# A decoder layer on one core: a second weight tile is multiplied during setup, and the first stage's small steps get new slots

## The chip, the cores and the metric

The kernel runs on one core of a Trainium2 chip. The metric is the device time of one execution in microseconds. Three runs of the kernel before took 1853.64, 1849.91 and 1853.60 us, median 1853.6. A difference of 0.2% is 3.7 us.

The engines: PE (TensorE) multiplies and writes PSUM, which has eight banks of 512 columns; ACT (ScalarE) and DVE (VectorE) read PSUM and SBUF; POOL (GpSimd) works in SBUF alone; SP (SyncE) issues most transfers.

## The reference

One inference step of one decoder layer, for a prompt of 1024 tokens and for 8 sequences of 4 tokens (the "samples"), 1056 columns in all, D = 1024:

```
ada = c @ w_ada + b_ada                      # shift, scale, gate for each norm
h = rmsnorm(x, g_norm1) * (1 + scale1) + shift1
z = h @ w_in                                 # q,k,v,o of two mixers, gates
qk = silu(causal conv of width 4 over q_a|k_a)
ha = mLSTM(q, k, v, input gate, log forget gate), normed per head
hb = gated linear attention(q, k, v, decays), normed per head
x = x + gate1 * ((sigmoid(g_a)*ha*sigmoid(o_a) + sigmoid(g_b)*hb*silu(r_b)) @ w_out)
x = x + gate2 * SwiGLU(rmsnorm(x, g_norm2) * (1 + scale2) + shift2)
```

All inputs and outputs are fp32. Each mixer has four heads. Outputs are the new x of both groups of tokens, normed, and the new states.

## The kernel before

**Products.** h is kept transposed, as eight chunks of 128 channels by 1056 tokens, and split in a high and a low part, each in the rounded fp32 format (`Hh`, `Hl`). So is every weight tile of 1024 x 128 (`Wh`, `Wl`). A product is Wh·Hh + Wh·Hl + Wl·Hh. A tile is multiplied in three thirds of the tokens (384, 320 and 352 columns, called pieces c = 0, 1, 2, one PSUM bank each) and two halves of the channels (h = 0, 1), so a half has 3 x 12 multiplications and a tile 72. Weights arrive as halves in four buffers (`raw`), ACT rounds a half to its high part (`split_hi`, L1326) and POOL subtracts to get the low part (`split_lo`, L1566).

**Setup** (`setup_phase`, L129 to L583). SP loads nine tiles of x rows, then `w_ada` in eight pieces of 1 MB (n = 0 to 7); behind piece 3 it issues four small strided loads for the tile "small" (gate columns and the rank-16 input), at the end the two halves of the weights of "q", and then it stores the transposed x. PE transposes x (L300), ACT squares its rows (L441) for the norm. PE multiplies the conditioning with each `w_ada` piece (`ada_part`, L337), ACT copies the sum out (`partial`, L447), PE turns it (`ada_columns`, L327). That happens four times, s = 0 to 3, and each gives shift and scale for two chunks of h. DVE then makes the multipliers (`affine`, L531), scales the chunk (`scaled`, L556: x times multiplier times the spread norm, which lies in PSUM), ACT adds the shift and rounds (`upper`, L454), DVE makes the low part (`lower`, L562). Between these, PE multiplies the first tile, "small", chunk by chunk as h is made (`first_upper`, `first_lower`, L350 and L362). Three times it multiplies the identity with itself instead (`keep_busy(8)`, L314).

**The mixer** (`mixer_phase`, L733) is a sequence of windows: S once, then A and B for each head, at the end L. Window S has the tiles small, q, k, v0, v1. A window's time is counted in slots, one slot for each piece of PE: `TIMELINE` lists piece after piece and, behind a piece, the small steps that `AT_SLOT` (L608) puts in that slot. Every engine goes through the same list in order and does its part of each entry. So the slot of a step is its place in each engine's queue. In S, slots 0 to 5 are small, 6 to 11 q, 12 to 17 k, 18 to 23 v0, 24 to 29 v1. ACT, at piece c = 0 of a half, splits the next half, and in the pieces of h = 1 it copies the finished bank out (`evacuate`, L1333). PE starts a tile's piece only when the bank's former content has been copied out (L1069 to L1070):

```
if h == 0:
    wait(pe, s_pfree[b], turns)
```

Banks 0 to 3 take turns by the number of the piece; small's pieces are 0 to 2, q's 3 to 5, k's 6 to 8, so k's second third lies in bank 3, where q's first was. The banks 4 to 7 serve the small steps.

**The small steps of S.** `rows` makes the rows of the gates: DVE adds the biases, ACT does exp and ln (L1424 to L1428), DVE sums and scans (`rows_stage`, L1949). `rows_exp` takes four exponentials on ACT (L1429). `rows_t` turns the rows on PE, DVE copies the columns, and SP stores the rows, which `decay_load` and `interq_load` read back. `conv_q`, `taps_q` and `silu_q` are the convolution (DVE), then tanh (ACT) and the product (DVE); the same for k. `vs0`, `vs1`, `vsum` are the values of the samples. Window A begins with its q tile; ACT and DVE make `decay` in slot 1 and ACT `alpha_hi` in slot 3.

Of the kernel before, what the change touches and what calls it, by code (L numbers as in the profile page):

```python
# [5 lines left out]
F32 = mybir.dt.float32  # L6
# [7 lines left out]
P = 128  # L14
# [114 lines left out]
def setup_phase(nc, g, a, block):  # L129

    with ExitStack() as ctx:
# [26 lines left out]
        ar = spare[:, 0:D].rearrange("p (j c) -> p j c", c=512)  # L158
# [14 lines left out]
        s_ssq, s_t, s_sqrt = sem("ssq_done"), sem("ms_done"), sem("sqrt_done")  # L173
# [6 lines left out]
        PARTB = (g.ps[4], g.ps[3])  # L180
# [10 lines left out]
        NQ = 256  # L191
        PARTS = [(0, 512), (512, 512), (SEQ, NS)]

        @block.sync
        def _(sp):
# [9 lines left out]
            for n in range(NA * KH):  # L205
# [15 lines left out]
            for h in range(2):  # L221
                sp.dma_start(g.raw[:, 2 + h], w_half(w_in, "S", 0, 1, h)).then_inc(g.s_w[2 + h], 16)
# [4 lines left out]
        def _(pool):  # L227
# [48 lines left out]
            pool.memset(g.nout[:, :], 0.0).then_inc(s_const, 1)  # L276
            for n in range(2):
# [3 lines left out]
            for n in range(2):  # L281
                pool.wait_ge(g.s_hi, n + 1)
                pool.tensor_tensor(g.Wl[:, n], by_parity(g.raw[:, n]), g.Wh[:, n].bitcast(F32), ALU.subtract).then_inc(g.s_lo, 1)

        @block.tensor
        def _(pe):
# [50 lines left out]
            def ada_part(n):  # L337
# [5 lines left out]
                if h == 0 and s >= 2:  # L343
                    pe.wait_ge(s_arow, s - 1)
                for k in range(KC // KH):
                    last = pe.matmul(PARTB[s % 2][CP * k:CP * (k + 1), :], cT[:, h * KC // KH + k, :], wpiece(n)[:, k, :],
# [3 lines left out]
            def first_upper(k, thirds):  # L350
# [3 lines left out]
                for m, w in enumerate((g.Wh, g.Wl)):  # L354
                    pe.wait_ge(g.s_lo if m else g.s_hi, h + 1)
                    for c in thirds:
                        if c == 2:
                            pe.wait_ge(g.s_hsh, h + 1)
                        pe.matmul(g.ps[c][:, 0:CUT[c + 1] - CUT[c]], slice_k(w[:, h], k % 4), g.Hh[:, k, CUT[c]:CUT[c + 1]],
                                  start=(k == 0 and m == 0), stop=False)  # L360

            def first_lower(k, thirds):  # L362
# [3 lines left out]
                for c in thirds:  # L366
                    if c == 2:
                        pe.wait_ge(g.s_hsl, h + 1)
                    last = pe.matmul(g.ps[c][:, 0:CUT[c + 1] - CUT[c]], slice_k(g.Wh[:, h], k % 4), g.Hl[:, k, CUT[c]:CUT[c + 1]],
                                     start=False, stop=(k == KC - 1))  # L370
                    if k == KC - 1 and c < NPC - 1:
                        last.then_inc(g.s_piece, 1)
                if k % 4 == 3 and 2 in thirds:
                    last.then_inc(g.s_used, 1)
            pe.wait_ge(s_trc, 1)
# [26 lines left out]
            first_upper(4, (0, 1))
            first_upper(5, (0, 1))
            ada_columns(3)
            for k in range(4):
                first_lower(k, (2,))
            first_lower(4, (0, 1))
            first_lower(5, (0, 1))
            keep_busy(8)
            first_upper(6, (0, 1))  # L410
            first_upper(7, (0, 1))
            for k in range(4, KC):
                first_upper(k, (2,))
# [2884 lines left out]
```

## Time and profile before

| | us |
|---|---|
| median of the three runs | 1853.6 |
| profiled execution, its span (first to last instruction) | 1851.7 |
| PE busy | 1815.7 |
| DVE, POOL, ACT busy | 1133.4, 776.4, 732.3 |

The profiled execution has no time of its own beside its span; what lies around the span is taken from the median of the runs. In the line of time of PE a multiplication of 128 columns and more is shown longer than its pitch, because multiplications are pipelined; the pitch is the difference of the starts. All times below are microseconds from the span's start.

### The profile page before, as it was taken

How to read it: one execution, taken by the hardware profiler on the slowest of the kernel's cores; microseconds unless marked ns; L12 is line 12 of the kernel's file. 1: busy time of each engine (PE TensorE's matmuls, PEld its weight loads, DVE VectorE, ACT ScalarE, POOL GpSimd, SP SyncE). 2: the span in 40 equal slices, each digit the busy share in tenths (PEclk: the TensorE clock that was granted, in tenths of full speed). 3: DMA queues.
4: the chain of work that ended last, by engine and by line, in shares of the span. 5: the costliest groups of instructions: out<-in, count | busy, mean ns of one | idle time of the engine just before them, and what ended most of it. 6: DMA issues, size and time to landing. Idle time of an engine off the chain costs nothing.

```text
span 1851.7 us, 36566 instructions
## 1 busy us (share of the span) xinstructions
PE 1815.7 (98%) x14652; PEld 1742.7 (94%) x14652; DVE 1133.4 (61%) x1960; ACT 732.3 (40%) x1528; POOL 776.4 (42%) x667
## 2 busy tenths in 40 slices
PE   7999999999999999999999999999999999999998
PEld 5899999999999999999989899989999999999998
DVE  6852746526474364753575688885675667566656
ACT  4543435344353443544435544223223222322327
POOL 4241434423344233432344773244345444544545
PEclk9999999999999999999999999999999999999999
DMA  9332231422224222232243741111112011111212
GB/s 314 118 98 58 78 92 53 137 63 78 87 58 130 64 83 82 58 122 66 83 140 96 216 127 57 46 46 51 43 46 69 26 58 56 58 35 46 69 47 95
DMA packets 182640, 154.82 MB, mean 84 GB/s; under 512 B 10324, under 2 KB 163092, under 8 KB 181960
## 3 DMA queue, kind: packets, MB, share of 16 engines
q1 hardware_dynamic: 182170, 152.27, 27.1%
q8 instruction: 117, 1.92, 0.4%
q14 instruction: 51, 0.42, 0.1%
q10 hardware_dynamic: 302, 0.22, 0.0%
HBM read 130.96 MB, written 21.50 MB: 82 GB/s over the span
## 4 chain that ended last, share of the span: by engine, by line
PE 80%; DVE 9%; POOL 3%; issue 3%; ACT 2%; DMA 2%; SPq 0%; ACTq 0%; DVEq 0%; POOLq 0%
PE bank L1076 24%; PE bank L2485 20%; PE bank L2454 12%; PE bank L1098 9%; PE bank L1243 3%; PE bank L2352 3%; PE bank L2319 1%; PE bank L1315 1%; POOL mix L1650 1%; PE bank L1223 1%; DVE gate L1906 1%; DVE y_rows L2918 1%; DMA x_rows<-in_w_ada 1%; PE bank L1296 1%; DVE y_rows L3099 1%
## 5 line engine op out<-in xcount | busy, mean ns | idle before, releaser
L1076 PE MATMUL bank<-h_hi,w_by_parity 128*128 128x320 f32 (+2 forms) x2304 | 449.0, 328 | 1.9 <-POOL w_by_parity L1574 1.9
L1574 POOL TENSOR_TENSOR w_by_parity<-w_raw,w_by_parity 128x512 fp32r<-128x512 f32 x128 | 193.3, 1510 | 530.0 <-ACT w_by_parity L1331 530.0
L1076 PEld LDWEIGHTS bank<-h_hi,w_by_parity 128*128 128x128 f32 x2304 | 378.1, 189 | 16.5 <-issue 11.2
L1076 PE MATMUL bank<-h_lo,w_by_parity 128*128 128x384 f32 (+2 forms) x1152 | 233.5, 324 | 0.0
L2784 POOL TENSOR_TENSOR f_by_parity<-w_raw,f_by_parity 128x512 fp32r<-128x512 f32 x107 | 145.7, 1367 | 196.1 <-ACT f_by_parity L2549 196.0
L2784 POOL TENSOR_TENSOR w_by_parity<-w_raw,w_by_parity 128x512 fp32r<-128x512 f32 x107 | 143.6, 1348 | 149.8 <-ACT w_by_parity L2549 149.8
L1076 PEld LDWEIGHTS bank<-h_lo,w_by_parity 128*128 128x128 f32 x1152 | 194.8, 189 | 0.0
L3133 DVE SCALAR_TENSOR_TENSOR x_t<-bank,ada,x_t 128x352 f32<-128x352 f32 (+1 forms) x288 | 155.8, 568 | 56.8 <-PE bank L2454 38.8
L1098 PE MATMUL bank<-w_by_parity,h_hi 128*128 128x256 f32 x1024 | 170.1, 281 | 1.0 <-POOL w_by_parity L1574 1.0
L2454 PE MATMUL bank<-act_hi,f_by_parity 128*128 128x352 f32 x528 | 155.0, 325 | 1.5 <-POOL act_lo L2818 1.1
L2454 PE MATMUL bank<-act_hi,w_by_parity 128*128 128x352 f32 x528 | 154.1, 323 | 1.4 <-DVE ffn_temps L2918 1.2
L1098 PEld LDWEIGHTS bank<-w_by_parity,h_hi 128*128 128x128 f32 x1024 | 140.9, 188 | 8.4 <-issue 7.0
L2549 ACT ACTIVATE f_by_parity<-w_raw 128x512 fp32r<-128x512 f32 x107 | 65.9, 626 | 136.0 <-DVE w_raw L2918 58.5
L2549 ACT ACTIVATE w_by_parity<-w_raw 128x512 fp32r<-128x512 f32 x107 | 65.9, 625 | 133.2 <-DVE w_raw L2918 51.6
L1331 ACT ACTIVATE w_by_parity<-w_raw 128x512 fp32r<-128x512 f32 x128 | 80.1, 626 | 81.1 <-PE bank L1076 57.6
L1098 PE MATMUL bank<-w_by_parity,h_lo 128*128 128x256 f32 x512 | 101.5, 279 | 0.0
L2454 PEld LDWEIGHTS bank<-act_hi,f_by_parity 128*128 128x128 f32 x528 | 97.5, 190 | 2.0 <-POOL act_lo L2818 1.4
L2454 PEld LDWEIGHTS bank<-act_hi,w_by_parity 128*128 128x128 f32 x528 | 96.6, 188 | 1.9 <-DVE ffn_temps L2918 1.9
L2485 PE MATMUL bank<-h_hi,w_by_parity 128*128 128x264 f32 x608 | 90.4, 283 | 0.8 <-DVE ffn_temps L3041 0.8
L2485 PE MATMUL bank<-h_hi,f_by_parity 128*128 128x264 f32 x608 | 90.1, 282 | 0.0
L2454 PE MATMUL bank<-act_lo,f_by_parity 128*128 128x352 f32 x264 | 85.6, 324 | 0.0
L2454 PE MATMUL bank<-act_lo,w_by_parity 128*128 128x352 f32 x264 | 85.1, 322 | 0.0
(570 smaller groups left out, 3779.9 us busy)
## 6 DMA issues: line engine op xcount, KB each, us to landing
w_raw<-in_w_in SPq DMA_DIRECT2D x128, 256.0 KB, 3.0
w_ada_tile<-in_w_ada SPq DMA_DIRECT2D x32, 512.0 KB, 4.2
w_raw<-in_w_out SPq DMA_DIRECT2D x48, 256.0 KB, 2.9
w_raw<-in_w_ffn_gate SPq DMA_DIRECT2D x44, 256.0 KB, 3.0
w_raw<-in_w_ffn_up SPq DMA_DIRECT2D x44, 256.0 KB, 3.0
w_raw<-in_w_ffn_down SPq DMA_DIRECT2D x44, 256.0 KB, 2.8
w_ada_ring<-in_w_ada SPq DMA_DIRECT2D x10, 512.0 KB, 9.6
x_scratch<-x_turned_rows SPq DMA_DIRECT2D x1, 4224.0 KB, 16.4
```

Source lines behind the costliest of these rows:

```text
L1076: last = pe.matmul(g.ps[b][:, 0:n], slice_k(x[:, s], k), y[:, 4 * h + k, c0:c0 + n], start=(h == 0 and k == 0 and m == 0), stop=(h == 1 an ...
L1098: last = pe.matmul(g.ps[b][:, t % 2 * DV:(t % 2 + 1) * DV], x[:, 2 * n + k, t * P:(t + 1) * P], y[:, s, :, k, :].rearrange("p a c -> p (a ...
L1223: last = pe.matmul(bank[s:s + NS, to:to + (NS if l == 1 else NS // 2)], KD[:, at:at + NS], qs, start=True, stop=True)
L1243: ins = pe.matmul(bank[:, 0:wide_], x[p][:, c * P:(c + 1) * P], y[r], start=(first and m == 0), stop=(final and m == 2))
L1331: act.activation(to, by_parity(raw[:, r]), ACT.Copy).then_inc(s_hi, 1)
L1574: pool.tensor_tensor(lo, by_parity(raw[:, r]), hi.bitcast(F32), ALU.subtract).then_inc(s_lo, 1)
L2352: last = pe.matmul(g.ps[bnk][:, 0:n], slice_k(x(s), kk), y[:, 4 * h + kk, c0:c0 + n], start=(h == 0 and kk == 0 and m == 0), stop=(h == 1 ...
L2454: last = pe.matmul(g.ps[bnk][:, 0:w], slice_k(x(s), r // 3), y[:, f, c0:c0 + w], start=(f == 0 and m == 0), stop=(f == 1 and m == 2))
L2485: last = pe.matmul(g.ps[bnk][:, 0:HQ], slice_k(x(s), kk), BLOCK[block][kk][y][:, q * HQ:(q + 1) * HQ], start=(m == 0 and kk == 0), stop=(m ...
L2549: act.activation(Wh(s), by_parity(made_of(n)), ACT.Copy).then_inc(s_hi, 1)
L2784: pool.tensor_tensor(Wl(s), by_parity(made_of(n)), Wh(s).bitcast(F32), ALU.subtract).then_inc(s_lo, 1)
L3133: dve.scalar_tensor_tensor(X[:, n, c0:c0 + m], g.ps[bnk][:, 0:m], g.ada[:, vec + n, 0:1], X[:, n, c0:c0 + m], ALU.mult, ALU.add).then_inc( ...
```

## The change

Setup multiplies two tiles, "q" first and then "small", in the banks 3, 6, 7 and 0, 1, 2. q's weights go to buffers 2 and 3 and are loaded behind `w_ada` piece 1. Two of three `keep_busy(8)` are gone. The copies of the partial sums and of the spread norm get places in `h_lo`'s last two chunks, and one bank serves all partial sums. ACT copies the spread norm to SBUF, and `scaled` is one instruction for all 1024 tokens. One root is taken ahead of the squares. In window S, the splits for small and q are gone from the list, and eight steps have other slots.

```diff
@@ sync
+                if n == 1:
+                    for half_ in range(2):
+                        sp.dma_start(g.raw[:, 2 + half_], w_half(w_in, "S", 0, 1, half_)).then_inc(g.s_w[2 + half_], 16)
...
-            for h in range(2):
-                sp.dma_start(g.raw[:, 2 + h], w_half(w_in, "S", 0, 1, h)).then_inc(g.s_w[2 + h], 16)
@@ gpsimd
+            first_lo(2, 1)
+            first_lo(3, 2)
             for n in range(2):
                 pool.wait_ge(g.s_w[n], 32)
...
+            first_lo(0, 3)
+            first_lo(1, 4)
@@ tensor
             ada_columns(0)
             ada_part(2)
+            upper_of("q", 0, (0, 1))
+            upper_of("q", 1, (0, 1))
             ada_part(3)
-            keep_busy(8)
+            both(lower_of, (0, 1), (0, 1), ("q",))
             ada_columns(1)
-            first_upper(0, (0, 1))
-            first_upper(1, (0, 1))
+            both(upper_of, (0, 1), (0, 1), ("small",))
             ada_part(4)
+            both(lower_of, (0, 1), (0, 1), ("small",))
             ada_part(5)
+            both(upper_of, (2, 3), (0, 1), ("q",))
             ada_columns(2)
+            both(upper_of, (2, 3), (0, 1), ("small",))
+            both(upper_of, range(4), (2,), ("q",))
             ada_part(6)
+            both(lower_of, (2, 3), (0, 1))
             ada_part(7)
+            both(upper_of, range(2), (2,), ("small",))
             ada_columns(3)
-            keep_busy(8)
+            both(upper_of, range(2, 4), (2,), ("small",))
+            both(upper_of, (4, 5), (0, 1))
+            both(lower_of, range(4), (2,))
+            both(lower_of, (4, 5), (0, 1))
+            both(upper_of, (6, 7), (0, 1), ("small",))
+            both(upper_of, range(4, KC), (2,), ("small",))
+            both(lower_of, (4, 5), (2,), ("small",))
+            both(lower_of, (6, 7), (0, 1, 2), ("small",))
+            both(upper_of, (6, 7), (0, 1), ("q",))
+            both(upper_of, range(4, KC), (2,), ("q",))
+            both(lower_of, (4, 5), (2,), ("q",))
+            both(lower_of, (6, 7), (0, 1, 2), ("q",))
@@ scalar
             act.wait_ge(s_t, 1)
+            act.activation(rstd[:, 0:1], ssq[:, 0:1], ACT.Sqrt).then_inc(s_sqrt, 1)
...
+            def rstd_row(b):
+                act.wait_ge(s_r, b + 1)
+                act.activation(RS[:, 512 * b:512 * b + 512], SPREAD[b], ACT.Copy).then_inc(s_sqrt, 1)
+            rstd_row(0)
             partial(0)
+            rstd_row(1)
+            weight(2)
+            weight(3)
             upper(0)
@@ vector
             def scaled(k):
-                for b in range(2):
-                    c0 = 512 * b
-                    ins = dve.scalar_tensor_tensor(HN[k][:, c0:c0 + 512], X[:, k, c0:c0 + 512], am[:, k, 0:1], SPREAD[b], ALU.mult, ALU.mult)
-                ins.then_inc(s_ht, 1)
+                dve.scalar_tensor_tensor(HN[k][:, 0:SEQ], X[:, k, 0:SEQ], am[:, k, 0:1], RS[:, 0:SEQ], ALU.mult, ALU.mult).then_inc(s_ht, 1)
@@ the slots of window S
-    "S": [("rows", 8), ("conv_q", 16), ("taps_q", 16), ("rows_exp", 17), ("silu_q", 19), ("vs0", 20), ("rows_t", 21), ("conv_k", 23),
-          ("taps_k", 24), ("silu_k", 25), ("decay_load", 25), ("interq_load", 25), ("vs1", 26), ("vsum", 27)],
+    "S": [("rows", 8), ("conv_q", 16), ("taps_q", 16), ("vs0", 20), ("rows_exp", 25), ("vs1", 26), ("rows_t", 27), ("vsum", 27),
+          ("silu_q", 27), ("conv_k", 28), ("taps_k", 28), ("decay_load", 28), ("interq_load", 28), ("silu_k", 29)],
@@ which half ACT and POOL split at a piece of S
+            if w == "S" and l < len(IN_SETUP):
+                return {(0, 1): ("S", 0, len(IN_SETUP), 0), (1, 0): ("S", 0, len(IN_SETUP), 1)}.get((l, h))
```

## Rows read from the trace of the kernel before

**Rows 1.** The page: busy us of each engine, its share of the span, instructions.
```profile
PE 1815.7 (98%) x14652; PEld 1742.7 (94%) x14652; DVE 1133.4 (61%) x1960; ACT 732.3 (40%) x1528; POOL 776.4 (42%) x667
```

**Rows 2.** Line of time, PE, setup: start, us, operation, count [idle before, releaser].
```profile
24.25 1.06 PE L346 MATMUL bank<-w_ada_ring,c_t 128*32 128x512 f32 x8 [1.25 <-DMA w_ada_ring<-in_w_ada]
...
26.63 1.06 PE L334 MATMUL bank<-group_sum,x_row_and_partials 128*128 128x9 f32 x8
...
30.20 1.90 PE L346 MATMUL bank<-x_rows,c_t 128*32 128x512 f32 x8 [1.51 <-DMA x_rows<-in_w_ada]
32.03 2.84 PE L317 MATMUL bank<-identity 128*128 128x128 f32 x16
...
50.44 1.95 PE L317 MATMUL bank<-identity 128*128 128x128 f32 x16
```

**Rows 3.** Stretches: length, busy of PE, PEld, DVE, ACT, POOL, PEclk, DMA, GB/s.
```profile
23.00:24.00 1.00, 0.00 (x0) 0.00 (x0) 0.00 (x0) 0.00 (x0) 0.00 (x0) 1.00 1.09 348
30.00:34.00 4.00, 3.80 (x18) 2.14 (x19) 3.54 (x4) 3.61 (x5) 2.05 (x3) 0.57 0.90 281
31.00:33.00 2.00, 2.00 (x12) 0.97 (x5) 1.98 (x3) 1.91 (x3) 1.18 (x1) 0.50 1.03 353
```

**Rows 4.** Line of time, PE, first stage.
```profile
57.03 0.86 PE L1076 MATMUL bank<-h_hi,w_by_parity 128*128 128x384 f32 x4
...
71.03 1.57 PE L1076 MATMUL bank<-h_hi,w_by_parity 128*128 128x384 f32 x8 [0.24 <-POOL w_by_parity L1574]
...
88.53 0.64 PE L1171 MATMUL bank<-w_raw,early 128*32 128x256 f32 x8 [1.34 <-ACT w_by_parity L1331]
...
90.85 0.74 PE L1098 MATMUL bank<-w_by_parity,h_hi 128*128 128x256 f32 x4 [1.01 <-POOL w_by_parity L1574]
```

**Rows 5.** Chain that ended last, 106 to 127 us: start, us, what, count.
```profile
106.46 3.70 PE bank L1098 x30
110.17 11.57 PE bank L1076 x72
121.74 5.61 PE bank L1098 x48
```

**Rows 6.** Line of time, ACT, setup to window A.
```profile
29.77 1.15 ACT L457 ACTIVATE h_hi<-early,ada 128x1024 fp32r<-128x1024 f32 x1 [3.80 <-DVE early L559]
...
60.69 0.46 ACT L1348 ACTIVATE v_b<-bank 16x352 f32<-16x352 f32 x1
...
67.45 1.09 ACT L1428 ACTIVATE temp_b<-temp_b 4x1056 f32<-4x1056 f32 x1
...
69.08 1.15 ACT L1356 ACTIVATE early<-bank 128x384 f32<-128x384 f32 x3
...
101.12 1.10 ACT L1450 ACTIVATE k_decayed<-early 128x1080 f32<-128x1080 f32 x1 [3.17 <-DVE early L1681]
...
113.25 1.06 ACT L1459 ACTIVATE temp_a<-temp_a 128x1024 f32<-128x1024 f32 x1 [1.87 <-DVE temp_a L1740]
...
118.61 2.18 ACT L1439 ACTIVATE alpha_inputs<-v_b 16x1056 fp32r<-16x1056 f32 x2
...
122.74 0.79 ACT L1361 ACTIVATE q_b<-bank 128x320 f32<-128x320 f32 x2
```

**Rows 7.** Line of time, DVE, setup to window A.
```profile
28.33 2.72 DVE L559 SCALAR_TENSOR_TENSOR early<-x_turned_rows,norm_mult,bank 128x512 f32<-128x512 f32 x4
...
84.24 0.16 DVE L1987 TENSOR_TENSOR m_ends<-m_ends 4x16 f32<-4x16 f32 x1
...
88.33 1.34 DVE L1681 SCALAR_TENSOR_TENSOR early<-early,vectors 128x1080 f32<-128x1080 f32 x1
90.84 0.73 DVE L1686 TENSOR_SCALAR early<-early 128x1080 f32<-128x1080 f32 x1 [1.17 <-ACT early L1450]
...
92.75 1.27 DVE L1689 TENSOR_TENSOR early<-early 128x32 f32<-128x32 f32 x1
...
109.82 3.23 DVE L1738 SCALAR_TENSOR_TENSOR temp_a<-temp_a,gate_cols,causal 128x128 f32<-128x128 f32 x8 [4.06 <-DMA temp_a<-gate_rows_scratch]
```

More of the change, by code:

```diff
@@ L342, in ada_part, with upper_of @@
                     pe.wait_ge(s_xc, 2 * NT)
-                if h == 0 and s >= 2:
-                    pe.wait_ge(s_arow, s - 1)
+                if h == 0 and s:
+                    pe.wait_ge(s_arow, s)
                 for k in range(KC // KH):
-                    last = pe.matmul(PARTB[s % 2][CP * k:CP * (k + 1), :], cT[:, h * KC // KH + k, :], wpiece(n)[:, k, :],
+                    last = pe.matmul(PARTB[CP * k:CP * (k + 1), :], cT[:, h * KC // KH + k, :], wpiece(n)[:, k, :],
                                      start=(h == 0), stop=(h == KH - 1))
                 last.then_inc(s_adau, 1)
-            def first_upper(k, thirds):
+            def upper_of(tile, k, thirds):
                 h = k // 4
                 pe.wait_ge(g.s_hh, k + 1)
-                for m, w in enumerate((g.Wh, g.Wl)):
-                    pe.wait_ge(g.s_lo if m else g.s_hi, h + 1)
+                for m in range(2):
+                    pe.wait_ge(g.s_lo if m else g.s_hi, MADE[tile] + h + 1)
                     for c in thirds:
@@ L368, in first_lower, with both @@
                         pe.wait_ge(g.s_hsl, h + 1)
-                    last = pe.matmul(g.ps[c][:, 0:CUT[c + 1] - CUT[c]], slice_k(g.Wh[:, h], k % 4), g.Hl[:, k, CUT[c]:CUT[c + 1]],
-                                     start=False, stop=(k == KC - 1))
+                    last = pe.matmul(g.ps[SETUP_BANKS[tile][c]][:, 0:CUT[c + 1] - CUT[c]], slice_k(g.W(0, HALF[tile] + h), k % 4),
+                                     g.Hl[:, k, CUT[c]:CUT[c + 1]], start=False, stop=(k == KC - 1))
                     if k == KC - 1 and c < NPC - 1:
                         last.then_inc(g.s_piece, 1)
-                if k % 4 == 3 and 2 in thirds:
+                if 2 in thirds and k == 3 and tile == "small":
                     last.then_inc(g.s_used, 1)
+                elif 2 in thirds and k == KC - 1:
+                    last.then_inc(g.s_used, 1 if tile == "small" else 2)
+            def both(f, ks, thirds, tiles=("q", "small")):
+                for tile in tiles:
+                    for k in ks:
+                        f(tile, k, thirds)
             pe.wait_ge(s_trc, 1)
@@ L591 @@
          "L": ["o0", "g0", "o1", "g1"]}
+IN_SETUP = ("small", "q")
+SETUP_BANKS = {"small": (0, 1, 2), "q": (3, 6, 7)}
 NS_TILES, NW_TILES = len(TILES["S"]), len(TILES["A"])
@@ L1328, in split_hi @@
                 act.wait_ge(s_w[r], turns * 16 + (16 + (32 if r < 2 else 0)))
-                wait(act, s_used, before - (SPL - 1))
+                wait(act, s_used, used_for(w, l, before))
                 to = halves_of_columns(Wh[:, s]) if TILES[w][l][0] == "v" else Wh[:, s]
@@ L1569, in split_lo @@
                 pool.wait_ge(s_hi, before + 1)
-                wait(pool, s_used, before - (SPL - 1))
+                wait(pool, s_used, used_for(w, l, before))
                 lo, hi = Wl[:, s], Wh[:, s]
```

85 lines of the change are left out of this document (40 added, 45 removed).

## The prediction

> **What bounds the kernel now.** I read the page first: PE is busy for 98% of the span [rows 1]. Only PE's idle, slowed and filler time can be given back, and only an engine that makes PE wait can cost anything. Then PE's own line of time through setup (to 57 us) [rows 2] and through the first stage (57 to 110 us) [rows 4], and ACT's and DVE's beside it [rows 6, 7]. The reader is to see three things. In setup PE waits for `w_ada` pieces and fills time with multiplications of the identity (`keep_busy`). From 57 us on it is dense but for two waits, at 88 and 91 us. ACT takes its work strictly in the order of the slot list, so one step that waits for DVE holds back every evacuation and weight split behind it.
>
> **Setup: what goes.** The second `keep_busy(8)` runs from 32.03 to 34.7 us and the third from 50.44 to 52.4 [rows 2]: 2.7 + 1.9 = 4.6 us. The wait of 1.5 us before 30.20 [rows 2] goes too, because its piece now has its turn on PE later, and I count 0.7 for two short waits for high halves of h.
>
> **Setup: what comes.** The "small" tile is still the first whose banks are emptied, but 48 of the 72 multiplications of "q" now stand ahead of its end; the last 24 follow it. 72 take 11.57 us [rows 5], 0.161 each, so 48 take 7.7. New waits: the two halves of q's weights (0.5 MB) now travel ahead of `w_ada` piece 2. The DMA engines are full there at 348 GB/s [rows 3], which makes 1.5 us. Piece 1 is waited for until 24.25 us [rows 2], and a piece is 1 MB or 3.0 us, so piece 2 lands near 28.7 instead of 27.2, while PE is free at 27.7 [rows 2]: 1.0 us. The first multiplication of q needs h's first high half. DVE starts scaling at 28.33 [rows 7] as before; a scaling of 1.3 us and ACT's 1.15 [rows 6] later it is 30.8, 1.1 us after PE is free again, and the second high half costs another 0.6. The low half of small's weights comes after two other splits on GpSimd: 0.6. Together 3.3 us. DVE is not the limit, since PE has 60 multiplications (9.7 us) between the last `ada_columns` and small's end. So "small" ends at 57.0 [rows 4] + 7.7 - 4.6 - 1.5 - 0.7 + 3.3 = 61.2 us, and q at 65.1. Bounds: 59.5 without the new waits for h, 62.5 if the half clock of rows 3 falls on useful work.
>
> **Small edits in setup.** Root's table load on ACT moves before the squares, and the root starts earlier by at most that load. But the spread norm is ready before `w_ada` piece 1, which PE awaits until 24.25 [rows 2]: 0 gained, and at most 0.3 lost if Square wanted a table of its own. Two ACT copies of the spread norm fall in ACT's idle time before 29.77 [rows 6]. Four scalings out of PSUM take 2.72 us [rows 7]; two long ones out of SBUF I put at 2.6, hidden behind PE. q's two weight splits on ACT stand ahead of the first high half of h: covered if the weights land before 28.4, and I put them at 25.8.
>
> **First stage: the wait that comes.** Order on ACT: evacuate "small", then `rows` (exp and ln of the gates, which wait for DVE), and only then evacuate q. Before, the last copy of "small" ended at 61.15, ln at 68.45, a weight split followed, and q's first copy ran from 69.08 to 69.57 [rows 6]. PE wanted that bank for the second third of "k" at 71.7 (71.03 and four multiplications) [rows 4], 2.1 us later: hidden. Now "small" ends at 61.2; its nine copies take 4.15 us, to 65.35; `rows` with ln takes 7.3 more, to 72.65; q's first copy 0.5, to 73.1 (the split is no longer between). PE is through q at 65.1 and through the first third of k at 67.4. It stands still for 5.7 us. The second third of k starts at 73.1 instead of 71.7: **+1.4 us**. All that setup gained is lost here, because this start follows the end of "small" by 11.9 us whatever PE has done meanwhile.
>
> **The clock.** After PE's idle time before 30.20 the granted clock is 0.50 from 31 to 33 us, 1.2 of 2.4 GHz, and 0.57 in the mean from 30 to 34 [rows 3]: 4 x 0.43 = 1.7 us of full clock lost, in 3.4 us at the lower level. It did not fall after the 1.3 and 1.0 us of rows 4. After 5.7 us of idling I expect the same once more, **+1.7 us** (bounds 0 and 1.7). The Trainium skill, "TensorE: Matmul & The Clock Gate", What's actually happening, calls the throttled state the default, which activity releases. The fall of rows 3 agrees with it; if it held for every idle stretch, rows 4 would show two more.
>
> **First stage: the waits that go.** `rows_exp` moves from slot 17 to 25, so ACT's splits for v0 and v1 no longer stand behind it. The waits of 1.34 us (88.53) and 1.01 us (90.85) [rows 4] go: **-2.4 us**. DVE's rows chain ended at 84.4 [rows 7] and now ends 4.2 us later, at 88.6; in slot 25, about 97 us, it is long done. The next window ("A") starts at 110.1 [rows 5] + 1.4 + 1.7 - 2.4 = 110.8.
>
> **The end of the stage and window A.** Here the moved steps meet. On ACT `silu_q` (slot 27) comes behind `vsum`; `conv_k` (28) and `silu_k` (29) follow. Counted from the end of `vsum` on PE (106.46 before [rows 5]): ACT copy 0.4, tanh 1.1 [rows 6]; DVE's silu, 90.84 to 94.0, 3.2; conv with taps, 84.4 to 89.7, 5.3 [rows 7]; tanh 1.1; and then the split of A's second q half, 0.6, which stands behind that tanh in ACT's order. With hand-overs 12.0. PE needs that half after 3.7 (to A's start) and 5.8 (36 multiplications) = 9.5: **+2.5 us**. Then window A's `decay`: DVE's silu_k 3.2 and decay 3.4 (3.23 [rows 7] and a short one), ACT's exps 1.2 (1.06 [rows 6] and a short one), split for v0 0.6, together 8.4 against PE's 0.6 + 5.8: **+2.0 us**. Then ACT copies q's first third (0.5), makes `alpha_hi` (118.61 to 122.74 [rows 6], 4.1) and copies the second third (0.4), whose bank v0 wants after 24 multiplications at 5.61/48 [rows 5], 2.8 us: 5.0 against 2.8, **+2.2 us**. Before, that copy came 1.3 us ahead of PE and the two splits 5 us. Behind v0's first half PE is again the slow one, and everything shifts with it. Bounds of the three together: 3 (ACT or DVE finds 1.2 us at each) to 9 (the clock falls once more, GpSimd and DVE slow one another).
>
> **Sum.** +1.4 + 1.7 - 2.4 + 2.5 + 2.0 + 2.2 = +7.4 us on the profiled span of 1851.7: 1859.1. The median of the runs, 1853.6, is 1.9 above that span, for what lies around it and one execution's luck: **1861.0**. The forecast's own range is 1857 to 1865.
>
> **Rivals.** (a) *PE's bookkeeping decides: faster.* If q's bank is empty when k wants it and the late steps don't bind, q ends 4.0 us earlier (65.1 for 69.1) and the two waits go: 1853.6 - 4.0 - 2.4 = 1847.2. For it: PE at 98%, DVE at 61% and ACT at 40% [rows 1]. Against it: ACT's order puts `rows` before q's copies, the margin was 2.1 us [rows 4, 6], and now PE comes 4 us earlier and the copy 3.5 us later. It decides from the point where q's copy ends before 67.4 us. Chance 0.14. (b) *The bank wait, without the tail: no change.* If conv and silu of k are done before PE needs ACT in window A, what is left is 1.4 + 1.7 - 2.4 = +0.7: 1854.3. For it: DVE had nothing to do for 4 us before `decay` [rows 7], so there was room; against it: slots 27 to 29 put 11.9 us of DVE and ACT work there. Chance 0.20. (c) *More of the same:* q's weights land late on ACT, or the clock falls twice more in window A, +3.4: 1864.4. Chance 0.10. The forecast keeps 0.56.
>
> **How the numbers follow.** A difference of 0.2%, 3.7 us, is what a measurement here can tell from none. Slower: the forecast but for its lower edge, and (c): 0.66 with a little of (b)'s upper side. Same: most of (b), and what of (a) and the forecast falls between: 0.19. Faster: (a), and a bit more: 0.15. The range 1851 to 1865 takes in (b), (c) and the forecast with its bounds; it leaves out (a) and some of what lies above (c), under 0.2 together.
>
> **What would show it.** Right: "small" ends on PE near 61 us; one PE wait of 5 to 6 us in k, near 67 to 73 us, put down to ACT's copy of q or to DVE behind it; the clock at 0.5 after it; no wait at `vs0`; then waits of about 2 us near 116, 124 and 129 us, put down to ACT. Wrong: k running through at 67 us (then (a) holds), or window A dense from its start (then (b)).

## The result, and the profile after

The changed kernel takes **1858.3 us** in the median of 8 runs (1856.1 to 1861.2), the kernel before 1852.1 us in 8 runs beside it (1849.8 to 1857.1): ratio **1.0036**, 95% interval 1.0027 to 1.0046. It is 6.2 us slower; 1861.0 (1851 to 1865) was predicted. The profiled execution has a span of 1857.2 us against 1851.7.

The page, the line that answers to [rows 1] (busy us of each engine, share of the span, instructions):

```profile
PE 1815.4 (98%) x14620; PEld 1742.0 (94%) x14620; DVE 1133.1 (61%) x1952; ACT 731.8 (39%) x1530; POOL 771.4 (42%) x667
```

It says nothing about 5.5 us. PE has 32 instructions fewer (the multiplications of the identity that went) and is as busy as before: part of its work ran at the lower clock (below). The places are seen on PE's line of time. The waits of PE from `w_ada` piece 2 to window A, without three of under 0.3 us, each in brackets behind the operation that had to wait (start, us, operation, count [idle before, releaser]):

```profile
28.56 1.07 PE L354 MATMUL bank<-w_ada_ring,c_t 128*32 128x512 f32 x8 [1.34 <-DMA w_ada_ring<-in_w_ada]
31.94 2.74 PE L369 MATMUL bank<-h_hi,f_by_parity 128*128 128x384 f32 x8 [2.32 <-ACT h_hi L472]
34.61 1.94 PE L354 MATMUL bank<-x_rows,c_t 128*32 128x512 f32 x8
...
63.67 2.74 PE L369 MATMUL bank<-h_hi,f_by_parity 128*128 128x384 f32 x16
...
75.72 1.43 PE L1111 MATMUL bank<-h_hi,w_by_parity 128*128 128x320 f32 x4 [5.45 <-ACT early L1393]
...
87.91 0.40 PE L1133 MATMUL bank<-w_by_parity,h_hi 128*128 128x256 f32 x2
...
113.26 0.87 PE L1111 MATMUL bank<-h_hi,w_by_parity 128*128 128x384 f32 x4
...
120.27 0.96 PE L1111 MATMUL bank<-h_hi,w_by_parity 128*128 128x384 f32 x4 [1.08 <-ACT w_by_parity L1368]
...
126.84 0.50 PE L1133 MATMUL bank<-w_by_parity,h_hi 128*128 128x256 f32 x2 [0.46 <-ACT w_by_parity L1368]
...
128.19 0.74 PE L1133 MATMUL bank<-w_by_parity,h_hi 128*128 128x256 f32 x4 [0.62 <-POOL w_by_parity L1611]
...
131.79 0.50 PE L1133 MATMUL bank<-w_by_parity,h_hi 128*128 128x256 f32 x2 [1.00 <-ACT q_b L1398]
...
134.71 1.95 PE L1159 MATMUL bank<-early 128*128 128x128 f32 x16
```

The reader is to see: the two waits of [rows 4] at 88 and 91 us are gone; in their place stand one of 5.45 us in k and four of together 3.2 us in window A. The last row, the scores of window A, is the best single mark. It stood at 127.19 us before (that row is quoted with the first experiment), so PE is **7.5 us** behind there. From 137 to 960 us the two traces run in parallel (7.5 to 7.7 us apart, by the starts of the same instructions on DVE). At the end 5.4 us are left. The lag changes at three places, far behind the edit. It is 6.4 us after 970: the clock of the kernel before falls in the stretch from 960 to 970 us (0.83), that of the changed kernel does not. It is 4.0 after 1040: the kernel before waits 1.69 us for a weight split at 1034.99 us, the changed one 0.16. It is 5.4 after 1260: from 1230 to 1250 us the changed kernel's clock is 1.00 and 0.66, that of the kernel before 0.93 and 0.90. The last is scatter of one execution, since the second profile of the changed kernel has no fall there (experiment 9); of the other two this is likely, but not shown. Over all kernels below that have several runs, the median of the runs lies 1722.4 to 1724.9 us above the start of the scores in the profile.

What PE waited for in k is on ACT's line of time, the rows that answer to the first half of [rows 6]:

```profile
63.56 0.48 ACT L1383 ACTIVATE mix<-bank 4x384 f32<-4x384 f32 x1 [4.17 <-PE bank L379]
...
67.79 0.63 ACT L1368 ACTIVATE w_by_parity<-w_raw 128x512 fp32r<-128x512 f32 x1
68.44 1.28 ACT L1463 ACT_TABLE_LOAD   x1
71.67 1.08 ACT L1463 ACTIVATE temp_b<-temp_b 4x1056 f32<-4x1056 f32 x1 [1.95 <-DVE temp_b L1997]
72.77 1.28 ACT L1465 ACT_TABLE_LOAD   x1
74.07 1.08 ACT L1465 ACTIVATE temp_b<-temp_b 4x1056 f32<-4x1056 f32 x1
75.17 1.15 ACT L1393 ACTIVATE early<-bank 128x384 f32<-128x384 f32 x3
```

q was complete on PE at 67.9 us, but its bank is read by ACT only at 75.17, behind `rows`, which itself waits 1.95 us for DVE. Before, the same copy ran at 69.08 [rows 6].

The clock, in stretches of 2 us (length; busy of PE, PEld, DVE, ACT, POOL; granted clock of PE; DMA share; GB/s), which answer to [rows 3]:

```profile
30.00:32.00 2.00, 0.06 (x1) 0.06 (x1) 1.98 (x3) 1.21 (x2) 0.04 (x1) 0.58 0.39 40
32.00:34.00 2.00, 2.00 (x7) 1.89 (x8) 2.00 (x2) 1.08 (x1) 1.14 (x2) 0.50 0.93 309
34.00:36.00 2.00, 2.00 (x11) 0.43 (x9) 0.45 (x1) 0.00 (x0) 0.00 (x0) 0.50 1.07 345
36.00:38.00 2.00, 2.00 (x14) 1.52 (x10) 0.00 (x0) 1.39 (x3) 0.19 (x1) 0.72 1.05 339
...
74.00:76.00 2.00, 0.28 (x1) 0.29 (x2) 0.82 (x1) 1.97 (x5) 0.00 (x0) 0.67 0.00 0
76.00:78.00 2.00, 2.00 (x8) 2.00 (x9) 1.97 (x2) 0.41 (x2) 0.00 (x0) 0.50 0.00 0
...
80.00:82.00 2.00, 2.00 (x10) 2.00 (x9) 2.00 (x9) 0.00 (x0) 0.00 (x0) 0.62 0.00 0
```

A mean of 0.58 over 2 us is 1.7 us at 0.50 (1.2 GHz) and the rest at 1.0 (2.4 GHz). So the clock is at the lower level from about 30.3 to 37.1 us, and again from 74.7 to 81.5: 6.8 us each time, of which 5.2 and 5.8 us fall on work that counts. Before it was low once, for 3.4 us [rows 3].

### The profile page after: what moved, and what is told of

Same layout as the page of the kernel before. It is cut to its first block, busy times and chain, and to the rows that moved or that the text cites. A ratio compares the mean times of both kernels' runs of the same rounds, so it can differ in the third digit from the quotient of the medians.

```text
span 1857.2 us, 36526 instructions
## 1 busy us (share of the span) xinstructions
PE 1815.4 (98%) x14620; PEld 1742.0 (94%) x14620; DVE 1133.1 (61%) x1952; ACT 731.8 (39%) x1530; POOL 771.4 (42%) x667
## 4 chain that ended last, share of the span: by engine, by line
PE 82%; DVE 9%; issue 3%; ACT 3%; POOL 2%; DMA 1%; ACTq 0%; SPq 0%; DVEq 0%; POOLq 0%
PE bank L1111 25%; PE bank L2522 20%; PE bank L2491 12%; PE bank L1133 10%; PE bank L1280 3%; PE bank L2389 2%; PE bank L2356 1%; PE bank L1352 1%; PE bank L2439 1%; POOL mix L1687 1%; DVE y_rows L3136 1%; PE bank L369 1%; PE bank L1260 1%; DMA w_ada_ring<-in_w_ada 1%; PE bank L1333 1%
## 5 line engine op out<-in xcount | busy, mean ns | idle before, releaser
L1111 PE MATMUL bank<-h_hi,w_by_parity 128*128 128x384 f32 (+1 forms) x2256 | 441.5, 329 | 8.2 <-ACT early L1393 5.5
L1611 POOL TENSOR_TENSOR w_by_parity<-w_raw,w_by_parity 128x512 fp32r<-128x512 f32 x126 | 186.3, 1479 | 537.7 <-ACT w_by_parity L1368 537.7
L1111 PEld LDWEIGHTS bank<-h_hi,w_by_parity 128*128 128x128 f32 x2256 | 371.1, 189 | 22.9 <-issue 11.7
L1111 PE MATMUL bank<-h_lo,w_by_parity 128*128 128x384 f32 (+1 forms) x1128 | 229.3, 325 | 0.0
L2821 POOL TENSOR_TENSOR w_by_parity<-w_raw,w_by_parity 128x512 fp32r<-128x512 f32 x107 | 144.0, 1351 | 150.7 <-ACT w_by_parity L2586 150.1
```

The lines of the kernel that those rows point to most:

```text
L1111: last = pe.matmul(g.ps[b][:, 0:n], slice_k(x[:, s], k), y[:, 4 * h + k, c0:c0 + n], start=(h == 0 and k == 0 and m == 0), stop=(h == 1 an ...
L1611: pool.tensor_tensor(lo, by_parity(raw[:, r]), hi.bitcast(F32), ALU.subtract).then_inc(s_lo, 1)
L2821: pool.tensor_tensor(Wl(s), by_parity(made_of(n)), Wh(s).bitcast(F32), ALU.subtract).then_inc(s_lo, 1)
```

## The experiments

Ratios are against the kernel before, run on the same chip beside them. "Scores" is the start of window A's scores on PE in the profile: 127.19 us before, 134.71 after. Slot lists are shown by the entries that differ. Theory: ACT's order causes all of the loss, at two separate places (`rows` ahead of q's copies, and the late slots ahead of window A), and the falls of the clock make the first dearer. Rival: the new setup itself costs it (one tile more to make before "small" is complete). "The values" are the first multiplications of v0, behind k. Where two kernels are compared in setup, times are counted from PE's first multiplication with `w_ada` piece 2, since that piece landed at 27.9 to 29.3 us in different executions.

**1. Old slot list in the changed kernel.**

```diff
-("rows_exp", 25), ("vs1", 26), ("rows_t", 27), ("vsum", 27), ("silu_q", 27), ("conv_k", 28), ... ("silu_k", 29)
+("rows_exp", 17), ("silu_q", 19), ("vs0", 20), ("rows_t", 21), ("conv_k", 23), ... ("silu_k", 25), ("vs1", 26), ("vsum", 27)
```

> The changed kernel with the first stage's slots of the kernel before. Mine: PE's 5.5 us wait in k and the low clock behind it stay (they belong to `rows` ahead of q's copies, slot 8 in both lists), the waits at the start of window A go (4.3 us between A's start and the scores), and of the waits near vs0 up to 1.5 us come back. The scores begin at 130.4 to 132 us instead of 134.7, and the kernel takes 1854 to 1855.5 us, 3 to 4 less than the changed one. Rival, the loss is all in setup and k and the slots carry none of it: 1858, no wait gone.

Measured: 1854.5 us, ratio 1.0016 (1.0008 to 1.0025). PE's line of time of this kernel has the wait in k, one short one behind it, and none in window A; beneath, the row of the kernel before that the marks are counted from:

```profile
74.92 1.43 PE L1111 MATMUL bank<-h_hi,w_by_parity 128*128 128x320 f32 x4 [5.45 <-ACT early L1393]
...
93.38 0.64 PE L1208 MATMUL bank<-w_raw,early 128*32 128x256 f32 x8 [0.38 <-ACT w_by_parity L1368]
...
113.85 0.87 PE L1111 MATMUL bank<-h_hi,w_by_parity 128*128 128x384 f32 x4
...
131.03 1.95 PE L1159 MATMUL bank<-early 128*128 128x128 f32 x16
```

```profile
127.19 1.95 PE L1122 MATMUL bank<-early 128*128 128x128 f32 x16
```

Window A's start to its scores takes 17.2 us here and 21.45 (113.26 to 134.71) with the new list. **The new list's tail costs 4.3 us.** From the values to window A it takes 26.6 us here (87.24 to 113.85) and 25.35 with the new list, so in the changed kernel the new list takes out 1.3 us and costs 3.0 net. The other 0.7 of the 3.7 us by which the scores come earlier here is an earlier `w_ada` piece 2 in this execution. And the waits that the new list was to remove are nearly gone without it (0.38 us is left of 2.35): PE comes to `vs0` some 5 us later than before, and ACT's splits are done by then.

**2. `rows` three slots later.**

```diff
-"S": [("rows", 8), ("conv_q", 16), ...
+"S": [("rows", 11), ("conv_q", 16), ...
```

> The changed kernel with `rows` in slot 11 instead of 8, so that ACT copies q out before it waits for the gates. Mine: the copy of q's first third runs near 68.5 us, k's second third starts near 70.1 us instead of 75.7, the clock stays at 1.0 there, and exp still starts at 71.7 because DVE sets it. 8.1 us less up to the end of k, window A's waits unchanged: scores at 126.6 us, kernel 1850 us. Rival, the wait only moves (to rows_exp and the splits, because DVE's rows end at 88.9 whatever PE does): scores no more than 3 us earlier, 1855 to 1858.

Measured: 1850.4 us, ratio 0.9995 (0.9986 to 1.0003): all of the loss is gone by one number. ACT's line of time of this kernel:

```profile
67.48 0.63 ACT L1368 ACTIVATE w_by_parity<-w_raw 128x512 fp32r<-128x512 f32 x1
68.14 1.15 ACT L1393 ACTIVATE early<-bank 128x384 f32<-128x384 f32 x3
...
69.40 1.28 ACT L1463 ACT_TABLE_LOAD   x1
```

q's copy runs at 68.14 instead of 75.17, PE has no wait in k, its clock stays at 1.00 through all stretches from 66 to 84 us, and the values start at 79.28 instead of 87.91. Window A keeps its four waits to the hundredth (1.08, 0.46, 0.62, 1.00): the two places are independent. Scores at 126.07, **8.6 us earlier**: 5.45 of wait, some 2.7 of clock, 0.3 of a better start, and 0.2 unassigned.

**3. The new slot list in the kernel before** (with its setup; DVE's wait for the sum's banks as in the change).

> The kernel before, with the new slots and the one wait that they need. Mine: the waits at 88 and 91 us go (2.4 us, at most 3.4), and window A's waits come (4.3 us as in the changed kernel), because they follow from the order silu_q, conv_k, silu_k behind vsum and not from setup: scores at 128 to 129 us against 127.2, kernel 1 to 2 us slower than before, 1853 to 1854. Rival, the tail comes from the late rows of the changed kernel alone: 2.4 to 3.4 us faster than before, 1849.

Measured: 1852.05 us, ratio 1.0003 (0.9995 to 1.0012), scores at 128.43, 1.2 us later than before; four waits in window A of 1.07, 0.46, 0.61 and 1.00 us. The mechanism and the mark are as expected; the time lies 1 us under its range, within what a run scatters. Put alone, the list adds 4.2 us ahead of the scores and takes out 3.2 between the values and window A (25.4 us instead of 28.6); the values start 0.2 later.

**4. A slot list of its own for the new order.** `rows` behind q's copies, `rows_exp` and `silu_q` before the crowd at slot 27, q and k's conv and silu apart.

```diff
-("rows", 8), ... ("rows_exp", 25), ("vs1", 26), ("rows_t", 27), ("vsum", 27), ("silu_q", 27), ("conv_k", 28), ("taps_k", 28), ...
+("rows", 11), ... ("rows_exp", 22), ("silu_q", 24), ("rows_t", 25), ("vs1", 26), ("conv_k", 26), ("taps_k", 26), ("vsum", 27), ...
```

> The changed kernel with rows in 11, rows_exp in 22, silu_q 24, rows_t 25, conv_k and taps_k 26 behind vs1, decay_load 27, silu_k 29. Mine: no wait in k, none near vs0, none in window A: A begins near 105.3 us and the scores near 122.5 us, against 110.0 and 127.2 in the kernel before; 1846 to 1848 us, 5 us faster than before. Rival, rows_exp in 22 holds ACT until DVE's rows end at 88.9 and the splits for v1 come late: 1850 to 1852.

Measured: 1848.3 us, ratio 0.9979 (0.9970 to 0.9989), 0.3 us above the expected range, scores at 123.82. From k's end to the scores PE waits once:

```profile
102.46 0.64 PE L1215 MATMUL bank<-early,group_sum 128*32 128x256 f32 x8 [0.64 <-DVE early L1747]
```

That wait, and a setup that began 0.7 us later in this execution (`w_ada` piece 2 at 29.22), are why the scores miss the expected 122.5.

**5. Multiplications of the identity in the setup wait.** They write a bank that is not yet in use. One `pe.matmul` of the identity shows as two multiplications in the trace, so `keep_busy(8)` is 16 there.

```diff
             ada_part(2)
+            keep_busy(8, g.ps[0])
             upper_of("q", 0, (0, 1))
```

> The changed kernel with eight identity products (2.05 us of PE) in the 2.3 us that PE waits between ada_part(2) and the first product of q. Mine: the idle time there is what makes the clock fall near 31 us, so it stays at 1.0; the eight products of q, ada_part(3) and the four low ones take 3.3 us instead of 5.8, less a wait of 0.6 for the second high half. Small ends 1.5 to 2.5 us earlier than 63.5, q's copy and k's second third follow it by the same, and the kernel takes 1.5 to 2.5 us less than the changed one: 1856. Rival, the waits near 23 and 27 us have already made it fall, or the fall costs nothing because ACT's high halves set the pace: small ends where it was, 1858.

Measured: 1857.6 us, ratio 1.0030 (1.0017 to 1.0043); the interval overlaps that of the change, so the time settles nothing. PE and its clock in this kernel, line of time and stretches:

```profile
29.14 1.06 PE L354 MATMUL bank<-w_ada_ring,c_t 128*32 128x512 f32 x8 [1.35 <-DMA w_ada_ring<-in_w_ada]
...
30.13 3.32 PE L325 MATMUL bank<-identity 128*128 128x128 f32 x16
33.10 1.98 PE L369 MATMUL bank<-h_hi,f_by_parity 128*128 128x384 f32 x8
```

```profile
30.00:32.00 2.00, 2.00 (x15) 1.87 (x12) 2.00 (x2) 0.69 (x1) 0.20 (x1) 0.67 0.51 57
32.00:34.00 2.00, 2.00 (x10) 2.00 (x10) 1.98 (x3) 1.61 (x2) 1.46 (x2) 0.50 0.67 213
34.00:36.00 2.00, 2.00 (x15) 0.95 (x13) 0.97 (x1) 0.00 (x0) 1.04 (x1) 0.98 1.06 361
```

**The clock was not kept up**, against the expectation: it fell at about 30.7 us, while these multiplications ran (3.32 us instead of the 1.95 of [rows 2]). PE's last idle time ahead of the fall is the 1.35 us before 29.14, so a wait before this one is enough for it, as the rival had it (it named the waits near 23 and 27 us). But it stayed low for 3.4 us, not 6.8, and most of that lay on the filling. k starts at 67.47 us, 1.0 us earlier than after, counted from `w_ada` piece 2. 1.5 to 2.5 had been expected; the filling ends 0.6 us later than PE had waited, which takes part of it back. Six profiles of this setup without filling have k 38.8 to 40.0 us behind that mark and this one 38.3, so between 0.5 and 1.6 us are the filling's. The shorter stretch comes again: the clock of setup was low for 3.4 us in all three kernels with this filling (5, 7, 11), and for 6.8 us in all seven profiles of the changed setup without it (the changed kernel twice, 1, 2, 4, 6, 10). What links the two is not shown. The second fall, behind the wait in k, was also shorter in this execution (3.4 us), which no part of the edit explains, so the scores at 133.07 can't be read as the filling's worth.

**6. The same in the wait in k.** 20 products, 40 multiplications in the trace, in front of the second third.

```diff
+if (w, *x[1:]) == ("S", 2, 0, 1):
+    for _ in range(20):
+        pe.matmul(g.ps[4][:, 0:P], g.ident[:, :], g.ident[:, :], start=True, stop=True)
 mm_piece(w, i, *x[1:])
```

> The changed kernel with twenty identity products (5.1 us of PE) in the 5.5 us that PE waits in k. It takes no wait away. Mine: k's second third starts where it did (near 75.5 us) and the clock stays at 1.0 behind it, so k ends 2.6 us earlier, and the kernel takes 2.6 us less than the changed one: 1855.5. Rival, the low clock after the wait was paid by something else that runs beside it (splits for v0 and DVE's rows), and the end of k does not move: 1858.

Measured: 1856.8 us, ratio 1.0026 (1.0016 to 1.0035). PE's line of time and the stretches behind the wait:

```profile
70.64 4.62 PE L1186 MATMUL bank<-identity 128*128 128x128 f32 x40
...
76.26 0.85 PE L1111 MATMUL bank<-h_hi,w_by_parity 128*128 128x320 f32 x4 [0.99 <-ACT early L1396]
...
85.85 0.40 PE L1133 MATMUL bank<-w_by_parity,h_hi 128*128 128x256 f32 x2
```

```profile
74.00:76.00 2.00, 1.27 (x12) 1.07 (x10) 0.28 (x1) 1.97 (x3) 0.00 (x0) 1.00 0.00 0
76.00:78.00 2.00, 1.74 (x12) 1.75 (x13) 1.97 (x2) 0.96 (x4) 0.00 (x0) 1.00 0.00 0
```

The wait is as long, the clock stays at 1.00, and from restart to the values it takes 9.6 us (76.26 to 85.85) instead of 12.2 (75.72 to 87.91). **The fall behind the wait costs 2.6 us**, shown by itself in the profile. The time does not show it: 1855.5 us was expected, and the interval overlaps that of the change. The setup of this execution took 0.6 us more (k starts at 68.46).

**7. Slot list of 4 with the filling of 5.**

> The kernel of e6_slots_anew with the filler of e3_filler_in_setup. Mine: the two gains add: 1.5 to 2.5 us less than 1848.3, 1846 to 1847. Rival, DVE's rows are the bound in the re-placed stage: small ends earlier, but vsum or a split waits for DVE and the time stays at 1848.

Measured: **1845.3 us, ratio 0.9968 (0.9957 to 0.9979)**: 6.2 us under the kernel before, and 0.7 under the expected range. The clock is low from 28.0 to 31.4 us only, k starts at 66.29, scores at 121.63. Of the 2.2 us that the scores gain on 4, 1.2 are an earlier `w_ada` piece 2 (28.00 for 29.22) and 1.0 goes with the filling, as in 5. By time the filling is worth 3.0 us here, with intervals that overlap.

**8. That kind of slot list with the old setup.** Slot list of 4, `rows` left in slot 8.

> The kernel before, with its own setup, and the slot list of e6_slots_anew (rows stays in slot 8, since here 'small' alone is made in setup). It tells how much of e7's gain the new setup carries. Theory: setup and k as before (values start near 81.4 us), the two waits at 88 and 91 us gone, perhaps 0.6 us before vsum as in e6, no wait in window A: scores at 127.2 - 2.35 + 0.6 = 125.4 us (124.8 to 125.6), time 1849.5 to 1850.5, 1.2 to 2 us above e6 and 4 to 5 above e7. Rival: the list alone gives all (its 3.4 us as in the changed kernel): scores near 123.8, time 1848.

Measured: 1849.2 us, ratio 0.9985 (0.9977 to 0.9994), scores at 124.89, as expected (the time 0.3 under its range; the 0.6 us before `vsum` did not come, and 0.67 us in k at 69.68 did, for ACT's split). It splits the gain of 7: the list alone gives 2.3 us by the scores, and the new setup with its filling another 3.3 (124.89 to 121.63; 3.1 by the ratios). Without the filling (4) it is 1.1 by the scores and 0.9 by the medians, which the runs can't tell from none. So the new setup is worth having with the filling; in the changed kernel the order on ACT spent it.

In this execution the clock of setup did not fall at all, with the same setup and the same wait, 1.50 us, for `w_ada` ahead of 30.19 us as in [rows 2]; the stretch to set beside [rows 3]:

```profile
30.00:32.00 2.00, 1.81 (x15) 0.97 (x16) 2.00 (x3) 1.83 (x2) 1.08 (x2) 1.00 0.69 184
```

"small" ends only 0.2 us earlier for it (k's first multiplication at 56.83 instead of 57.03), because PE then waits 1.35 us for `w_ada` at 39.17.

**9. The changed kernel once more**, unedited, for a second profile.

> The changed kernel as it is, for a second profile. Two falls of the clock are expected, behind PE's waits near 29 to 32 us and 70 to 76 us. If the length at the lower level is chance (3.4 or 6.8 us in the kernels so far), one of them may last 3.4 us here, and the scores come at 131.3 or 133.0 instead of 134.7 us; if it is set by the order of the work, both last 6.8 us and the scores come at 134.5 to 135 us. The waits in window A are as before in either case: 1.1, 0.5, 0.6 and 1.0 us.

Measured: 1856.1 us in one run, scores at 134.09. The wait in k is again 5.45 us and both stretches at the lower level are again 6.8 us long, but they begin earlier: by the same reckoning from the stretches at 29.0 and 73.4 us instead of 30.3 and 74.7, so that more of each lies ahead of PE's restart: 1.9 us more in setup and 1.3 in k. What the first gives, 0.55 us, a later `w_ada` piece 2 (29.11) takes back, so that k starts at 67.91 again; the second gives 0.6 us, and the scores come 0.6 earlier than in the first profile, 0.4 under the expected 134.5. The stretches in which the two begin:

```profile
28.00:30.00 2.00, 0.89 (x8) 0.20 (x8) 1.93 (x4) 0.10 (x1) 2.00 (x2) 0.75 1.04 273
72.00:74.00 2.00, 0.00 (x0) 0.00 (x0) 0.00 (x0) 1.98 (x2) 0.00 (x0) 0.84 0.01 3
```

In both profiles the clock fell while PE stood, but here 1.3 us earlier by the time since the span's start, with the same instructions. Of the two expectations the second holds for the lengths and the waits; only the scores lie outside it. In the old setup the length was not the same (3.4 us in [rows 3], 6.8 in experiment 3, none in 8).

**10. GpSimd's second split behind DVE's first scaling.** It asks why the first high half of h came late.

```diff
 first_lo(2, 1)
+pool.wait_ge(s_ht, 1)
 first_lo(3, 2)
```

> The changed kernel, but GpSimd makes the second low half of q's weights only after DVE's first scaling of x (one wait more on GpSimd). In the changed kernel the two splits ran from 27.13 to 29.62 us and DVE's first scaling, which reads two operands in SBUF, took 2.24 us, the seven others 1.28. Theory: the two instructions exclude each other. Then norm_mult still takes 0.78, the first scaling takes 1.28, GpSimd's second split starts when it ends, ACT's first high half comes 1.0 us earlier, PE's wait for it is 1.3 instead of 2.3 us, and k starts 1.0 us earlier counted from w_ada piece 2 (38.3 us behind it instead of 39.35, if the clock falls alike). Rival: the first scaling is slow for a reason of its own (first use of the operands): then nothing changes, and the wait stays at 2.3 us.

GpSimd and DVE in the changed kernel:

```profile
27.13 2.49 POOL L283 TENSOR_TENSOR f_by_parity<-w_raw,f_by_parity 128x512 fp32r<-128x512 f32 x2 [6.96 <-ACT f_by_parity L482]
```

```profile
27.65 0.78 DVE L563 SCALAR_TENSOR_TENSOR norm_mult<-ada,vectors 128x18 f32<-128x18 f32 x1
28.46 3.44 DVE L581 SCALAR_TENSOR_TENSOR early<-x_turned_rows,norm_mult,rstd_rows 128x1024 f32<-128x1024 f32 x2
```

and GpSimd, DVE and PE in this kernel:

```profile
27.32 1.27 POOL L283 TENSOR_TENSOR f_by_parity<-w_raw,f_by_parity 128x512 fp32r<-128x512 f32 x1 [7.09 <-ACT f_by_parity L483]
30.02 2.26 POOL L283 TENSOR_TENSOR f_by_parity<-w_raw,f_by_parity 128x512 fp32r<-128x512 f32 x1 [1.43 <-DVE early L582]
```

```profile
28.66 2.48 DVE L582 SCALAR_TENSOR_TENSOR early<-x_turned_rows,norm_mult,rstd_rows 128x1024 f32<-128x1024 f32 x2
```

```profile
31.18 2.73 PE L370 MATMUL bank<-h_hi,f_by_parity 128*128 128x384 f32 x8 [1.39 <-ACT h_hi L473]
```

The two scalings take 2.48 instead of 3.44 us, PE's wait is 1.39 instead of 2.32, and k starts 38.4 us behind `w_ada` piece 2 instead of 39.4. Counted from `w_ada` piece 2, PE restarts after 2.46 us; in six profiles without this edit (the changed kernel twice, 1, 2, 4, 6) it is 3.27 to 3.47. **A split of GpSimd and a scaling of DVE, which reads two operands in SBUF, kept each other out**: the one that came second took 1.0 us longer, DVE's first scaling in the changed kernel (2.24 us for 1.28) and GpSimd's second split here (2.26 for 1.27). The Trainium skill, "SBUF — State Buffer", Who interferes with whom, calls the port pair that the two share an exclusive lock; these rows agree with it. Whether it gains anything at the scores this one run can't show: they come at 134.14 us, and at 134.09 in the second profile of the unedited kernel.

**11. Everything together**: 7 and 10, with 10 multiplications of the identity instead of 16.

> The slot list and filling of e7_slots_and_filler, GpSimd's second split after DVE's first scaling as in e10, and 10 multiplications of the identity instead of 16, so that the filling ends when the first high half is ready. k started 38.29 us behind w_ada piece 2 in e7; if the splits were in DVE's way, it is 0.8 to 1.3 us less here, and the scores come at 120.4 to 120.9 us for the same landing of piece 2 (28.0 us); time 1844 to 1845. If not, PE waits 0.6 us behind the shorter filling and all marks are those of e7: 1845.3.

Measured: 1844.5 us, **ratio 0.9955 (0.9942 to 0.9969)**, in 5 runs against 9 of the kernel before. k starts 37.6 us behind `w_ada` piece 2, 0.7 less than in 7, just short of the expected 0.8. Scores at 122.18, above the expected 120.4 to 120.9; here piece 2 landed 1.3 us later than in 7 (29.30). Over 7 the gain is seen in the profile; by time the two can't be told apart.

The marks side by side, all in us of the profiled execution but the last column:

```
                           k starts  values   A starts  scores   median
before                       57.0     81.4     110.0    127.2    1852.1
changed                      67.9     87.9     113.3    134.7    1858.3
1 old slot list              67.1     87.2     113.9    131.0    1854.5
2 rows in slot 11            67.6     79.3     104.6    126.1    1850.4
4 slot list anew             68.6     80.2     106.6    123.8    1848.3
6 filling in k               68.5     85.9     111.2    132.6    1856.8
7 list of 4, filling         66.3     78.1     104.4    121.6    1845.3
8 list of 4, old setup       56.8     82.0     107.7    124.9    1849.2
9 changed, again             67.9     87.3     112.7    134.1    1856.1
11 everything                66.9     78.6     105.0    122.2    1844.5
```

## Why the prediction was right, step by step

The mechanism, the places and the sum were right: +7.4 us to the scores predicted, 7.5 measured. That the two agree so closely is luck. The terms erred in both directions: the start of k's second third by +2.6 us, the clock behind it by +0.9, the waits that go by -0.8, window A by -2.4. At the end of the span +5.5 us is left and the medians differ by 6.2, so the time, 1858.3 for 1861.0, is met less closely; 1.5 us of that miss lie in the base, 1853.6 us from three runs where eight give 1852.1.

- **Setup, mis-sized: "small" ends at 63.6 us** (ACT's first copy starts at 63.56), 6.6 later than before; +4.2 (61.2) was predicted. Two terms. The wait for the first high half was 2.3 instead of 1.1 us: I took a scaling at 1.3 us whatever GpSimd did beside it, and they stood in each other's way (experiment 10). And the stretch at the lower clock, which before fell on one `ada_part` and on filling [rows 2, 3] and cost 0.2 us in the end (experiment 8), now falls on q's multiplications: 8 take 2.74 us instead of 1.5, `ada_part` 1.94 instead of 1.06, and with the four of the low half behind them it is 5.6 us from start to start (31.94 to 37.52) for some 3.1, 2.5 us more. I had it as a bound only (62.5), and sized that bound by the 3.4 us of [rows 3]; it lasted 6.8. The other new waits were shorter than priced (second high half 0 for 0.6, low half 0.24 for 0.6, and `w_ada` piece 2 at 28.56 for 28.7).
- **The wait in k, right in place and mechanism**: one wait of 5.45 us (5.7 predicted), put down to ACT's copy of q, behind `rows`. The restart follows "small"'s end by 12.1 us (11.9). So it inherits setup's error: 75.72 instead of 73.1, **+4.0 instead of +1.4 us**. This is the largest miss, and the reason that all of setup's 6.6 us matters while q's end, 1.2 us earlier than before, does not. Experiment 2 shows that ACT's order alone does it.
- **The clock behind it: +2.6 us instead of +1.7**, outside my bounds of 0 and 1.7. I assumed the length of [rows 3] again. The cost itself is shown by experiment 6.
- **The two waits that go: -3.2 us instead of -2.4** (from the values' start to window A 28.57 before, 25.35 after). 2.35 are the rows in brackets. By the starts in the two traces the same two waits take 2.7 us: a bracket counts from the shown end of the multiplication before, which is later than its pitch. The other 0.5 is that `rows_t` and `vsum` interrupt the values twice before (at 92.60 and 105.82 us) and once after (108.37); the forecast had no term for that. Experiment 1 shows that the two waits would have all but gone anyway once PE came late.
- **Window A, mis-sized: +4.3 instead of +6.7**. All three waits stand at the pieces where they were predicted (they end at 120.3, 126.8 to 128.2 and 131.8 us; 116, 124 and 129 were given for a window that began 2.5 us earlier), on ACT and once on GpSimd behind it, with 1.08, 1.1 (0.46 and 0.62) and 1.00 us in their rows. By the starts of PE the first costs 1.2 us where 2.5 were predicted and the second 0.6 where 2.0 were. The third was right: from v0's start to its second bank it is 4.95 us (126.84 to 131.79) for the 5.0 of the working, 2.1 more than PE's own 2.8, and the 0.62 us for GpSimd lie inside it. In the first two DVE was quicker than the rows that I took: silu of q 2.1 instead of 3.2 us (111.20 to 113.30), decay 2.18 instead of 3.23. Silu of k still took 3.1 (119.73 to 122.79), beside a split at 120.30. Those rows of before [rows 7] had a split on GpSimd beside them, the same exclusion as in experiment 10:

```profile
91.68 2.29 POOL L1574 TENSOR_TENSOR w_by_parity<-w_raw,w_by_parity 128x512 fp32r<-128x512 f32 x1 [0.88 <-ACT w_by_parity L1331]
```

  is the kernel before; DVE's operation of 32 columns at 92.75 ends with it, after 1.27 us. After, with GpSimd idle (its splits are at 106.48 and 120.30), the same one takes 0.19:

```profile
113.11 0.19 DVE L1726 TENSOR_TENSOR early<-early 128x32 f32<-128x32 f32 x1
```

- **Rival (a)**, PE's own account decides: refuted for the changed kernel, and true for experiment 2, where the copy comes before k wants the bank. **Rival (b)**, no tail: refuted by the four waits. **Rival (c)**, a second fall of the clock: half true, since there were two long ones, but none in window A.

By price, from the experiments: the order of `rows` costs 8.6 us (2), the new slots 4.3 against the 1.3 (1) or 3.2 (3) that they take out, and the new setup with a filling is worth 3.3 us once neither stands in its way (8 against 7; 1.1 without the filling, 8 against 4). **Left open:** what decides whether, when and for how long the clock falls in setup, why the stretch was shorter with the filling, and 2 us of scatter behind the scores.

## What to carry to other kernels

Making a second tile early moves a bank's hand-over, not only PE's work: before changing what PE does first, write down the order of the engine that empties the banks, and move its steps that wait for others behind the copies that free banks. A slot list is tuned to one order of work; a bad neighbour in it cost here more than the whole edit could bring, and one number gave it back. Filling multiplications can be worth keeping even when work is there to replace them, if a slow stretch of the clock would otherwise fall on that work (3.4 us instead of 6.8 in setup, 2.6 us saved in k).

## What the runs showed of the hardware

- Stretches at the lower clock behind one wait lasted 3.4 us or 6.8 us, in kernels with the same setup (kernel before, experiment 3), and once there was none (experiment 8, with a wait of 1.50 us). In the changed setup it was 6.8 us in all seven profiles without filling and 3.4 in all three with it. The sentence that the prediction took from the Trainium skill, "TensorE: Matmul & The Clock Gate", What's actually happening, agrees with the falls after waits, but the run with the same wait and no fall shows that a wait alone does not tell.
- In experiment 5 the fall came while PE was multiplying 128x128 identities; with 40 of them in the longer wait in k (experiment 6) it did not come.
- A split on GpSimd and an instruction of DVE that reads two operands in SBUF exclude each other per instruction: 1.27 us became 2.26 on GpSimd, 1.28 became 2.24 and 0.19 became 1.27 on DVE.
